# Feed-forward's up products with the weights as stationary operand

## The reference

```
a, v = split(h @ w_up, 2)          # w_up: 2048 x (2 * 5504)
a    = conv3x3(a, grid 4 x 64) + conv_b    # per channel, 9 taps
out  = (silu(a) * v) @ w_down      # w_down: 5504 x 2048
x    = rmsnorm(x + gate * out) * g_final
```

## Time and profile before

| | us |
|---|---|
| time, median of 3 runs | 2165.66 (2165.31 to 2165.68) |
| the profiled execution's own time | 2165.97 |
| its span | 2164.3 |
| TensorE busy in the span | 2113.7 (98%) |
| VectorE busy | 1507.3 (70%) |
| ScalarE busy | 1047.0 (48%) |

### The profile page before, as it was taken

How to read it: one execution, slowest core, us unless ns; L and a number is a source line. 1 busy time by engine, 2 the same in 40 slices (tenths; PEclk the granted TensorE clock), 3 DMA queues, 4 the chain that set the end, 5 groups by cost and what they waited for, 6 DMA issues and landing times.

```text
span 2164.3 us, 28673 instructions
## 1 busy us (share of the span) xinstructions
PE 2113.7 (98%) x9993; PEld 1723.2 (80%) x9993; DVE 1507.3 (70%) x2244; ACT 1047.0 (48%) x1296; POOL 53.9 (2%) x103
## 2 busy tenths in 40 slices
PE   7999999999999999999999999989999999999998
PEld 6777878788887777877788887868888888888886
DVE  5466667867677887787665877567777877775555
ACT  5444435554444444446534554445554555554443
POOL 0000000000001000000000000000000000000000
PEclk9999999999999999999999999989999999999999
DMA  8887878978787979876444446655565555667664
GB/s 311 279 282 264 281 236 302 331 255 279 266 292 259 332 232 346 312 263 211 137 136 121 119 115 225 199 185 183 176 199 173 184 191 175 193 192 243 196 191 141
DMA packets 281624, 487.42 MB, mean 225 GB/s; under 512 B 21918, under 2 KB 113152, under 8 KB 279472
## 3 DMA queue, kind: packets, MB, share of 16 engines
q1 hardware_dynamic: 276176, 467.98, 65.8%
q0 software_dynamic: 5344, 18.05, 2.4%
HBM read 479.49 MB, written 6.48 MB: 225 GB/s over the span
## 4 chain that ended last, share of the span: by engine, by line
PE 85%; DVE 7%; issue 3%; ACT 3%; DMA 2%; SPq 0%; DVEq 0%; ACTq 0%
PE gemm_ps L1854 72%; PE ps L1854 4%; DVE w_lo L1062 2%; DVE msum L1226 2%; ACT w_hi L636 2%; PE ps L1892 1%; DMA w_raw<-in_w_in_dram 1%; PE ps L2253 1%; DMA w_raw<-in_w_out_dram 1%; DVE tmpT L1094 1%; PE ps L2391 1%; PE ps L2322 1%; PE ps L1933 0%; PE ps L2276 0%; PE ps L2275 0%
## 5 line engine op out<-in xcount | busy, mean ns | idle before, releaser
L1062 DVE TENSOR_TENSOR w_lo<-w_raw,w_hi 128x1024 fp32r<-128x1024 f32 (+1 forms) x688 | 827.9, 1215 | 455.9 <-ACT w_hi L636 449.0
L636 ACT ACTIVATE w_hi<-w_raw 128x1024 fp32r<-128x1024 f32 (+1 forms) x688 | 710.7, 1051 | 476.2 <-PE gemm_ps L1854 331.4
L1854 PE MATMUL gemm_ps<-w_hi,a_hi 128*128 128x512 f32 (+1 forms) x2176 | 865.0, 397 | 18.6 <-DVE w_lo L1062 10.5
L1854 PE MATMUL gemm_ps<-w_hi,a_lo 128*128 128x512 f32 (+1 forms) x2176 | 847.1, 389 | 0.0
L1854 PE MATMUL gemm_ps<-w_lo,a_hi 128*128 128x512 f32 (+1 forms) x2176 | 846.2, 389 | 0.0
L1854 PEld LDWEIGHTS gemm_ps<-w_hi,a_hi 128*128 128x128 f32 x2176 | 409.9, 188 | 124.2 <-issue 25.0
L1854 PEld LDWEIGHTS gemm_ps<-w_hi,a_lo 128*128 128x128 f32 x2176 | 409.7, 188 | 86.6
L1854 PEld LDWEIGHTS gemm_ps<-w_lo,a_hi 128*128 128x128 f32 x2176 | 410.4, 189 | 79.5 <-issue 0.5
L1756 DVE SCALAR_TENSOR_TENSOR acc<-gp,cw,acc 128x256 f32<-128x256 f32 x344 | 151.4, 480 | 13.8 <-DVE acc L1756 1.4
L1226 DVE SCALAR_TENSOR_TENSOR msum<-mraw,cs,msum 128x1024 f32<-128x1024 f32 x120 | 153.3, 1278 | 0.7
L1854 PE MATMUL gemm_ps<-w_hi,ft_hi 128*128 128x512 f32 x344 | 134.2, 390 | 2.2 <-DVE w_lo L1062 2.2
(11 more groups left out here) (405 smaller groups left out, 1551.0 us busy)
## 6 DMA issues: line engine op xcount, KB each, us to landing
w_raw<-in_w_in_dram SPq DMA_DIRECT2D x336, 512.0 KB, 4.6
mraw<-in_w_mod_dram SPq DMA_DIRECT2D x192, 512.0 KB, 6.2
w_raw<-in_w_up_dram SPq DMA_DIRECT2D x336, 256.0 KB, 3.1
w_raw<-in_w_down_dram SPq DMA_DIRECT2D x84, 512.0 KB, 4.3
w_raw<-in_w_out_dram SPq DMA_DIRECT2D x64, 512.0 KB, 5.2
w_raw<-in_w_up_dram SPq DMA_DIRECT2D x24, 512.0 KB, 5.2
x_d<-xres POOLq DMA_DIRECT2D x2, 2048.0 KB, 8.4
gate_bias<-in_b_gate_dram SPq DMA_DIRECT2D x12, 256.0 KB, 6.6
```

The source lines that it names most:

```text
L636: act.activation(w_hi[:, slot, :, 0:n], raw[:, slot, :, 0:n], ACT.Copy).then_inc(hi_done, 1)
L1062: dve.tensor_tensor(w_lo[:, slot, :, 0:n], raw[:, slot, :, 0:n], w_hi[:, slot, :, 0:n].bitcast(F32), ALU.subtract).then_inc(lo_done, 1)
L1854: mm = pe.matmul(out[:, rt, 0:n], x[:, chunk0 + k, rt * P:(rt + 1) * P], w[:, slot, kk, 0:n], start=(k == 0 and part == 0), stop=(k == chu ...
```

## The change

TensorE's `ffn_block` no longer calls `product`. Weights are the stationary operand (128 x 128 of a unit), the activations stream (128 x 256), and an output of 128 channels x 256 positions goes to a bank of its own: four banks of `gemm_ps` for even blocks, the four of `ps` for odd ones. The transposes, `ub` and its copy are gone. ScalarE and VectorE read the banks directly; all of a block's convolution now stands in the block behind it, at earlier places, and its `ft_lo` one block later still. From block 2 on a block waits for `f_fv` of the block before; so does the down product, for block 21's.

```
-            def turn_u(b, par, nf):
-                pe.wait_ge(evac_act, 42 + b)
-                if not (isinstance(b, int) and b == 1):
-                    pe.wait_ge(S("f_fv"), b - 1)
-                ...
-                            mm = pe.transpose(bank[:, f * T + rt * P:f * T + (rt + 1) * P], ub[:, 1 - par, rt, c0:c0 + P], ident)
+            def ffn_block(b, par, n=2):
+                first = isinstance(b, int) and b == 0
+                if first:
+                    pe.wait_ge(evac_dve, 20)
+                    for g in range(2):
+                        turn("x2", y, 0, g)
+                elif not (isinstance(b, int) and b == 1):
+                    pe.wait_ge(S("f_fv"), b - 1)
+                for i in range(BU):
+                    slot = i % SLOTS
+                    ...
+                    pe.wait_ge(lo_done, U_FFN + BU * b + i + 1)
+                    for kk in range(UK):
+                        k = UK * i + kk
+                        for half in range(2):
+                            for f in range(n):
+                                out = (ps[:, 2 * half + f] if par else gemm_ps[:, half, f])[:, 0:T]
+                                c0 = (half * n + f) * P
+                                for part, (w, x) in enumerate(((w_hi, a_hi), (w_hi, a_lo), (w_lo, a_hi))):
+                                    mm = pe.matmul(out, w[:, slot, kk, c0:c0 + P], x[:, k],
+                                                   start=(k == 0 and part == 0), stop=(k == KC - 1 and part == 2))
+                    mm.then_inc(used, 1)
+                    ...
-            ffn_block(21, 1, n=T)
+            ffn_block(21, 1, 1)
             pe.wait_ge(S("f_lo"), 20)
             for c in range(DC):
                 if c < 2:
-                    pe.wait_ge(evac_act, 63 + c)
+                    pe.wait_ge(S("f_fv"), FB - 1)
```

ScalarE (its `conv`; `up_rows` picks the banks), and the same places on VectorE:

```
+                if i == 3:
+                    act.wait_ge(used, U_FFN + BU * b)
+                    src = up_rows(par, 0, n).rearrange("p f (y x) -> p f y x", y=4)
+                    ...                       # gp, first tap, as before at i == 6
+                if i == 7:
+                    act.wait_ge(S("f_acc"), b)
+                    act.activation(sil[:, 0:n], acc[:, 0:n], ACT.Silu).then_inc(S("f_sil"), 1)
+                if i == 9:
+                    act.wait_ge(S("f_fv"), b)
+                    act.activation(ft_hi[:, bass.ds((b - 1) * 2, n)], fv[:, 0:n], ACT.Copy).then_inc(S("f_hi"), 1)
-                act.activation(ub[:, par], gemm_ps[:, par], ACT.Copy).then_inc(evac_act, 1)
```

```
+                if 4 <= i < 7:
+                    ...
+                    for tap in {4: (1, 2, 3), 5: (4, 5, 6), 6: (7, 8)}[i]:
+                    ...
+                if i == 8:
+                    value = ps[:, 2:2 + n, 0:T] if par else gemm_ps[:, 1, 0:n, 0:T]
+                    dve.wait_ge(S("f_sil"), b)
+                    dve.tensor_tensor(fv[:, 0:n], sil[:, 0:n], value, ALU.mult).then_inc(S("f_fv"), 1)
     ...
+                        if i == 2 and behind:
+                            low_part(b - 1, 2)
+                        conv(b, i, 1 - par, 2)
```

More of the change, by code:

```diff
@@ L33 @@
 FCH = FF // P
+DOWN_LATER = 3
 GDV = 256
@@ L982, in _, with up_rows, conv @@
                 last_square(rt, xres, lambda rt: y[:, rt, (DC - 1) * NBLK:DC * NBLK], 1)
[L985 to L996, removed]
+            def up_rows(par, half, n):
+                if par:
+                    return ps[:, 2 * half:2 * half + n, 0:T]
+                return gemm_ps[:, half, 0:n, 0:T]
+            def conv(b, i, par, n):
+                if i == 3:
+                    act.wait_ge(used, U_FFN + BU * b)
+                    src = up_rows(par, 0, n).rearrange("p f (y x) -> p f y x", y=4)
+                    for f in range(n):
                         ins = act.activation(gp[:, f, 1:5, 1:65], src[:, f], ACT.Copy)
                     me(ins)
-                    for f in range(start):
+                    for f in range(n):
                         fc = (b - 1) * 2 + f
@@ L1015, in ffn_block @@
                     splits(U_FFN // SLOTS + 2 * b, i, i + 1, ffn=True)
[L1016 to L1019, removed]
-                act.activation(ub[:, par], gemm_ps[:, par], ACT.Copy).then_inc(evac_act, 1)
-            ffn_block(0, 0, 0, 0)
+                    if not first:
+                        conv(b, i, 1 - par, 2)
+            ffn_block(0, 0)
             act.wait_ge(S("gp_zero"), 2)
-            ffn_block(1, 1, 2, 0)
+            ffn_block(1, 1)
             first = me.n
@@ L1737, in _, with low_part, conv @@
             roots()
[L1740 to L1750, removed]
+            def low_part(b, n):
+                dve.wait_ge(S("f_hi"), b)
+                at_f = bass.ds((b - 1) * 2, n)
+                dve.tensor_tensor(ft_lo[:, at_f], fv[:, 0:n], ft_hi[:, at_f].bitcast(F32), ALU.subtract).then_inc(S("f_lo"), 1)
+            def conv(b, i, par, n):
+                if 4 <= i < 7:
+                    if i == 4:
                         dve.wait_ge(S("f_tap0"), b)
-                    for tap in {7: (1, 2, 3), 8: (4, 5, 6), 9: (7, 8)}[i]:
+                    for tap in {4: (1, 2, 3), 5: (4, 5, 6), 6: (7, 8)}[i]:
                         dy, dx = tap // 3, tap % 3
-                        for f in range(start):
+                        for f in range(n):
                             a_f = acc[:, f].rearrange("p (y x) -> p y x", y=4)
@@ L1773, in ffn_block @@
                     splits(U_FFN // SLOTS + 2 * b, i, i + 1)
-                    ffn_hook(b, i, par, start, finish)
-            ffn_block(0, 0, 0, 0)
+                    if not first:
+                        if i == 2 and behind:
+                            low_part(b - 1, 2)
+                        conv(b, i, 1 - par, 2)
+            ffn_block(0, 0)
             dve.memset(gp[:], 0.0).then_inc(S("gp_zero"), 1)
-            ffn_block(1, 1, 2, 0)
+            ffn_block(1, 1, False)
             dve.wait_ge(S("x2_out"), 16)
```

41 lines of the change are left out of this document (15 added, 26 removed).

## The result

The changed kernel takes 2175.06 us (median of 5 runs, 2172.83 to 2178.34), the kernel before 2165.68 us beside it (2165.31 to 2166.86): ratio 1.0041 [1.003, 1.0052]. Forecast were 2174.9 and a range of 2170.5 to 2182. The changed kernel's five runs spread over 5.5 us; what separates those at 2176 to 2178 from its trace can't be read from it.

A forecast was written before the change was run, and what follows sets the result against it. TensorE's instruction count times their spacing was taken as the bound. Terms +25.6 + 1.3 - 19.5 + 1.8 = +9.2 us gave 2174.9 us against the median of 2165.66, range 2170.5 to 2182.

The forecast's parts named there:

- spacing: Blocks 1 to 20: 192 matmuls of 256 columns at 0.120 us replace 96 of 512 at 0.2267; +25.6 us.
- turning: Transposes removed from blocks 1 to 21 and the first down block: 0.91 us per loop block, 19.5 us saved in all.
- Block 0: First feed-forward block: 96 more matmuls paying 0.0133 us each; +1.3 us.
- Block 21 and its handover: Last block into down products: transposes save 0.88 and 0.45 us, TensorE's waiting for VectorE adds 1.8.
- the three named: TensorE's waits in block 21 for units 6 and 7 and at the down start, 4.3 us lost in all.
- restarts: Some 0.3 us added to the 4.3 us of waits between block 21 and the down products.
- Cheap halves: Rival: in blocks 0 to 20 the second matmul on the same weights skips its 0.0133 us; 17.9 saved, 2157; chance 0.03.
- Issue as the bound: Rival: loop matmuls step slower than 0.120 us; at 0.125, 20 us more (2195), at 0.135, 60 more; chance 0.06.
- Clock at the handover: Rival: waits after block 21 drop the granted clock to 0.50, costing 2 to 4 us more, 2177.3; chance 0.10.
- Vector work: Rival: the loop's 19.1 us chain to the gated product overruns by over 3.9 us; 2195 at 1 over; chance 0.03.
- the 3.9 us of cover: In the loop, the gated product is done at 19.1 us, TensorE asks at 23.04; so no cost expected.
- Little or no change: Rival: the handover's loss vanishes and transposes were worth some tenths more per block; sum under +4.3 us; chance 0.05.

The follow-up runs named there:

- the kernel without turning: The kernel before with its 172 transposes removed, so its values are not the reference's: 2147.75 us, ratio 0.9917.
- the repeat: The changed kernel run again unaltered, against the kernel before: 2173.38 us, ratio 1.0034.
- the first one-load kernel: Changed kernel with each three matmuls' first two joined into one of 512 columns, VectorE adding the halves: 2176.89 us, ratio 1.0054.
- the kernel with both edits: Changed kernel with high-weight matmul pairs joined (ScalarE's tap after its split), and block 20's last convolution moved into the first down block: 2156.85 us, ratio 0.9952.

## Why the prediction was right

The mechanism was right: 96 more instructions a block at their fixed cost outweigh the transposes that go. Every step is put beside its term, from the two profiled executions.

- Products of blocks 1 to 20: +25.6 expected for spacing and -18.2 for turning, +7.4 together. Measured 460.80 after; before, the same blocks took 453.39 (from 1450.76 to 1904.15): +7.41. The two halves of this sum were each tested: the kernel without turning gives -19.1 against -19.5 for the whole, and a steady 0.120 is in the loop.
- Block 0: +1.3 expected, +0.4 measured (28.03 from its first matmul to that of block 1, against 27.61). This is the term that was mis-sized: I charged 0.0133 for each of its 96 more matmuls, 0.16 a unit of 12 more. The two traces' TensorE has the end of the first unit, where the next work, four transposes, begins, here before (with the first matmul of block 1) and then after:

```profile
1428.44 0.61 PE L1933 MATMUL ps<-cst,xn 128*128 128x128 f32 x4
...
1450.76 0.39 PE L1854 MATMUL gemm_ps<-w_hi,a_hi 128*128 128x512 f32 x1
```

```profile
1427.14 0.38 PE L2412 MATMUL gemm_ps<-a_hi,w_hi 128*128 128x256 f32 x1
1427.36 0.28 PE L2412 MATMUL gemm_ps<-a_lo,w_hi 128*128 128x256 f32 x1
1427.48 0.28 PE L2412 MATMUL gemm_ps<-a_hi,w_lo 128*128 128x256 f32 x1
1427.59 0.60 PE L1943 MATMUL ps<-cst,xn 128*128 128x128 f32 x4
```

  The first unit takes 5.29 us before (from 1423.15) and 5.09 after (from 1422.50): -0.20 in place of +0.16. While the clock is at 0.50, 256 columns step by 0.2133 and 512 by 0.4267, which is columns over 1.2 GHz with nothing beside, so that the added matmuls cost nothing; and after, the step falls to 0.12 before the unit is over, as before it doesn't. That second part is chance: in the two other traces of the changed kernel the first unit takes 5.29 too, and the granted clock rises later. The second unit takes 2.86 before (1428.80 to 1431.66) and 2.95 after (1427.95 to 1430.90), +0.09 in place of +0.16, since before it stepped by 0.23 there and not by 0.2267. Over the traces block 0 was 28.03, 28.64 and 28.31 us long in the changed kernel, 27.25 and 28.16 in the two others with the same block 0, and 27.61, 27.30 and 27.75 in three with the old one: by the means +0.5, while traces of one form differ by up to 0.8 from their mean, by the moment at which the clock rises.
- Block 21 and its handover: 0.88 and 0.45 of turning less, and 1.8 more of idle time, +0.5 together. Measured +1.90 up to the first down product (15.79 against 13.89) and then -1.68. The first down product started 15.79 after the block against 15.8, 4.27 us above 96 x 0.120 where 4.3 was worked out, and its three waits were the three named. The 0.3 that I added for restarts was in the 4.3 already: VectorE's chain decides when the down product starts, and a restarted matmul inside block 21 (0.22 in place of 0.12) only takes from the wait behind it. Before had lost part of its own behind the down start (0.98), so that this appears there as a gain. The sum, +0.2, is 0.2 to 0.3 under the one expected, about those restarts.
- Ahead of the feed-forward the profiled execution was 0.65 us shorter (first matmul 1422.50 against 1423.15), which no step of mine has. The three traces of the changed kernel have that matmul at 1422.50, 1423.69 and 1421.55, so 0.65 is less than one program differs from itself there.

Together: -0.65 + 0.42 + 7.41 + 1.90 - 1.68 = +7.4, the difference of the spans, where +9.2 was worked out. The medians differ by 9.4; their extra 2 us lie in executions of which there is no trace, so that the median falls 0.2 from the forecast is partly luck. In the repeat the medians differ by 7.5, as the two traces do.

The rivals. Cheap halves: the second of each three has a load of its own for the same tile (193 loads to 194 matmuls in the window of block 3), and its step is 0.120 like the others; what a second use without a load would cost, no run shows. Only one instruction of 512 columns saves anything, and it saves just the 0.0133. Issue as the bound: fell, as 3,840 pairs of load and matmul held 0.120; the 0.135 that I took as an upper bound was counted from the end of a split at 1907.22, while TensorE came to the unit that needed it only at 1908.46. Clock at the handover: stayed at 1.00 in all three traces of the changed kernel. Vector work: the loop's product, of which 19.1 us after the block's first matmul was worked out, ends 19.1 after it in block 4 (which begins at 1519.65), so the 3.9 us of cover are there:

```profile
1538.05 0.68 DVE L1767 TENSOR_TENSOR fv<-sil,ps 128x512 f32<-128x512 f32 x1
```

How thin the cover of the splits is shows in the first one-load kernel, where 1.4 us of additions on VectorE, one more copy on ScalarE and ScalarE's wait for the sum were enough to make them late. Little or no change: not what came, as the medians differ by 9.4 and 7.5, and the intervals of both ratios lie above 1.002.

The Trainium skill's rule that I set against the trace ("TensorE: Matmul & The Clock Gate", section "Back-to-back issue gap", columns over 2.4 GHz plus 2.5 ns) would have had the change win some 13 us. The measured step keeps 13.3 ns beside the columns at the full clock, for 256 columns, for 512, and for 512 + 256 as a pair twice that in three traces (0.3467 = 0.3200 + 2 x 0.0133) and more in a fourth. At the lower clock nothing beside the columns was measured, as the section has it for a cold engine.

## What to carry to other kernels

Where TensorE is the bound, count its instructions by the measured step of their shape: which operand is stationary decides how many columns each load serves, and removing work of the layout (here 0.91 us of transposes a block) pays only if it is more than the steps it adds (96 x 0.0133 = 1.28). When two products share a stationary tile, put their moving sides into one instruction, but first see that the engine that must add the halves has the time in its place in the queue. Where a stage gets shorter than the queue of work behind it, as block 21 does here, move that work past the handover: 4 us here for no instruction more. In the kernel before, where the same remedy had 2 us to win, the times couldn't tell it from nothing.

## What the hardware showed that I had not expected

- The cost beside the columns is there at the full clock (0.0133 us) and not at the lower one (0.2133 for 256 columns, 0.4267 for 512).
- A matmul with its load steps by 0.111 us at the full clock with 128 columns moving and by 0.112 with 4, so the columns don't set it; at the lower clock it is 0.2133 with 128. 256 columns (0.120) are just above it at the full clock, so narrower tiles gain nothing. Eight transposes cost eight such steps.
- 128-column matmuls from block 0 on ran 1743 us at a granted clock of 0.50 with TensorE shown busy throughout; the same matmuls in block 20 alone, behind blocks at 1.00, stayed at 1.00 for their 42 us. TensorE did the same thing in both; before, it had been idle for 8.0 us in the one and busy in the other.
- The step of a 512 and 256 pair was 0.3467 us in three traces and 0.3533 in one of the same form, each time throughout the blocks without waits. Open.
- Behind 24 matmuls of 4 columns the granted clock stood at 0.50 from about 986 to 989.5 us in one trace of the changed kernel, and for a stretch behind the same matmuls in the slower of the two traces of the kernel with both edits, while TensorE was shown busy; it stayed at 1.00 there in the other two traces of the changed kernel, and in the quicker trace of the kernel with both edits. Like the 128-column matmuls, these are narrow ones with a load each. Why it falls in some executions only is open.
